# Down groups of 8, 4, 4, 8, 8 tiles, weights split ahead of a stage's end, and a third ordinary pair in the third MLP

## Chip, cores and metric

The kernel runs on one core of one Trainium2 chip. The metric is device time in microseconds, the median of several executions.

## The reference, cut to what matters

Three transformer blocks follow one another on a sequence of 1024 tokens with 1024 channels, all in float32. The change touches the MLP of the first and of the third block, what stands just ahead of the third one, and the small product `w_ada` that runs beside the first one's down projection:

```
# block 1
h = h + square(relu(rms_norm(h, norm_mlp_w) @ w_up)) @ w_down        # 1024 -> 4096 -> 1024
# block 3
mod = silu(c) @ w_ada + b_ada                                        # 6 vectors of 1024, from w_ada (1024, 6144)
x = x + gate1 * rms_norm(mix, norm1_post)
h = rms_norm(x, norm2_pre) * (1 + scale2) + shift2
f = square(relu(h @ w_fc1)) @ w_fc2                                  # 1024 -> 4096 -> 1024
x = x + gate2 * rms_norm(f, norm2_post)
```

## The kernel before

Channels lie on the 128 partitions and tokens along the rows, so that an activation is eight tiles k of 128 x 1024. A weight tile of 128 x 1024 produces 128 output channels. Each float32 product is made of three products of split operands: with `hi` the operand rounded by ScalarE (ACT) and `lo` the rest, TensorE sums hi*hi, hi*lo and lo*hi. For weights ACT writes `whi` (`highs`, a list in the order of use; L1404) from `raw`, and GpSimd (POOL) writes `wlo` in the place of `raw` (`lows`, L3043). `whi` has two buffers, `raw` four.

**The engines' queues** are written out by hand, one function for each engine. An instruction that waits holds up everything behind it in its function. `behind(name)` on SyncE (SP) loads the weights four ahead, once TensorE has released the buffer.

**Up projection of both MLPs.** The 32 tiles of the hidden layer come as 16 pairs (`pair_of`). The first pairs are ordinary ones (`job`): a tile is 8 k x 6 = 48 matmuls of 512 columns, a pair 96. The other pairs are fast ones (`fast`, L746 to L748): a product of 2 x 2 blocks with seven block products p1, p5, p6, p4, p7, p2, p3 instead of eight, 84 matmuls. The fast pairs need sums of activations, made once (operands p5, p6, p4, p7: `operands1`, `operands2`, `operand_lows`), and sums of weights for each pair (`fast_sums` on DVE, `fast_hi` on ACT, `fast_lo` on GpSimd, L3113). Results are put together by `fast_step` on DVE, squared on ACT and written to memory (`spill`, tensor `hsc`). Before, pairs 0 and 1 are ordinary in both MLPs. `drain` multiplies an ordinary tile by the norm's factor RT and squares it on DVE; in the third MLP a `relu` with a bias on ACT stands between. PSUM has three slots of 128 x 1024 in turn, and a fourth tile `misc` for sums and for the norms' factors.

**Down projection** (`down`, `dn` in block 1, `fa2_` in block 3). The 32 hidden tiles are taken in five groups of `SIZES` = 8, 8, 8, 4, 4 tiles. For each group there are eight steps, one for each output tile, so 40 steps n. A step is 48 matmuls in a group of 8 and 24 in a group of 4; DVE adds its result to X. Even groups stand in GH/GL, odd ones in HH/HL. During a group's steps the next group's tiles come back from memory, one in a step (`next_tile`): SP issues `reload`, ACT makes the high half (`high_down`), GpSimd the low half. On ACT the step's order is the weights of step n + 1 and then the high half of the reloaded tile; on GpSimd it is the same. The first group's tiles are reloaded during the last fast pair; their low halves 0, 2, 4, 6 are made by GpSimd, 1, 3, 5, 7 by DVE (`low_down`), 5 and 7 of them behind the last `fast_step`.

**The product with w_ada** runs beside the first MLP's down steps. `ADAS[n]` lists the rows (of 48) that step n carries: two in each of the first 24 steps. A row is a DMA of 512 KB into one of three buffers, eight dependent DVE operations of 128 x 128 (`row_step`, L2475 and L2110) and one small matmul, which TensorE issues a step later. SP's order is

```
for n in range(40):
    ...
    down("up", n)
    for f in ADAS[n]:
        if f + 3 < 48:
            row_load(f + 3)        # waits for "red ada f", the end of row f on DVE
```

and `down` issues the reload of step n, then the weights of step n + 4, which wait for TensorE's end of step n.

**The end of the first MLP.** Behind its last down step follows tile gg0 of the second block, whose weights ACT splits behind the squares of `on_last3` (`behind("gg0")`).

**The start of the third MLP.** `halves` runs fa1_0, fa1_1, fa1_2 in two halves of 512 tokens, with the sums of squares (`sums_half`, L769) and the transposes that spread the factors (`spread_half`, L776) between. Behind them follow the sums and both spreads of norm `nx`, then fa1_3, then the fast pairs. On DVE all operands of the fast pairs are made between the norm's last sum and `factors_half("nx", 1)` (L2916).

Of the kernel before, what the change touches and what calls it, by code (L numbers as in the profile page):

```python
# [16 lines left out]
P = 128  # L17
# [257 lines left out]
def build(nc, d, out):  # L275
    ctx = ExitStack()
    with ctx:
# [164 lines left out]
        ring = [name for name in cut if name != "fa1_1" and name not in SPLIT]  # L442
        ridx = {name: i for i, name in enumerate(ring)}
        WX = at("WX", RO, [P, 1024], R)
        HXF, HF, GF = unit("HXF", HO, 0, [P, 8, S]), unit("HF", HO, 8, [P, 8, S]), unit("GF", GO, 8, [P, 8, S])
# [8 lines left out]
        def whi_of(name):  # L454
            n = int(np.prod(wl[widx[name]][1].shape[1:]))
            if name == "fa2_4_7":
                return whi[ridx[name] % 2][:, n:2 * n]
# [4 lines left out]
            return (WX if name == "fa1_1" else whi[ridx[name] % 2])[:, 0:n]  # L462

# [22 lines left out]
        def wh_of(t, w):  # L486

            return at_whi[(ridx[f"{t}2"] + w % 4 // 2) % 2][w % 2]
# [9 lines left out]

        def corners(t, n):
# [4 lines left out]
        def hidden(n):  # L504

            return TB[2 * (n % 2)], TB[2 * (n % 2) + 1]
# [122 lines left out]
        def tensor(e):  # L629
# [35 lines left out]
            def begin(name, hi, lo, toks, nk, k0=0, m=P, ks=None, between=None):  # L665
# [9 lines left out]
                def step(n):  # L675
# [21 lines left out]
                    elif n == 3 and name in ("up3", "fa1_3"):  # L697
# [29 lines left out]
            def fast(t, n):  # L727
# [3 lines left out]
                for j, p in enumerate(PARTS):  # L731
# [7 lines left out]
                    elif n > 2:  # L739
                        q.wait_ge(*dv({"p1": f"{t}c11 {n - 1}", "p5": f"{t}c12a {n - 1}", "p6": f"{t}u3 {n - 1}", "p4": f"{t}c21a {n - 1}"}[p]))  # L740
                    wh, wl_ = wh_of(t, 7 * (n - 2) + j), part(t, n, p)[1]
                    for k in range(4):
                        if n == 2 and p in OAT:
# [8 lines left out]
            def fast_all(t):  # L752
# [3 lines left out]
                for n in range(2, 16):  # L756
# [587 lines left out]
            def next_norm(name, hf, k):  # L1344
# [5 lines left out]
                elif (name, hf, k) == ("fa1_0", 1, 4):  # L1350
                    sums_half("nx", 0, 0, dv("nx acc7 h0"), dv("mixn 7 0"))

            halves(["fa1_0", "fa1_1", "fa1_2"], hhs, hls, lambda k, hf: [dv(f"hl6 {k} {hf}")], 8, between=next_norm, along=True)
            sums_half("nx", 1, 512, dv("nx acc7 h1"), dv("mixn 7 1"))
            spread_half("nx", 0, misc, dv("nx r1 h0"))
            spread_half("nx", 1, misc, dv("nx r1 h1"))

            def tail(name, hf, k):
# [3 lines left out]
                elif (name, hf, k) == ("fa2_4_6", 1, 1):  # L1362
                    spread_half("nf", 0, misc, dv("nf r1 h0"))

            job("fa1_3", hhs, hls, lambda k: [], 8)
# [3 lines left out]
            halves(["fa2_4_5", "fa2_4_6", "fa2_4_7"], ghs, gls, lambda k, hf: [either(f"fa2_l {FIRST[4] + k}")], 4, between=tail)  # L1369
# [10 lines left out]
        def scalar(e):  # L1380
# [5 lines left out]
            def highs(upto):  # L1386

                while todo and widx[todo[0]] <= upto:
# [3 lines left out]
                    if name == "fa1_1":  # L1392
                        q.wait_ge(*dv("zu3"))
                    elif name == "fa2_4_7":
                        q.wait_ge(*pe("fa2_4_3"))
# [91 lines left out]
            def fast_hi(t, w):  # L1487

                n, p = w // 7 + 2, PARTS[w % 7]
# [7 lines left out]
                if w > 3:  # L1497
                    q.wait_ge(*pe(f"{t}{(w - 4) // 7 + 2} {PARTS[(w - 4) % 7]}"))
                else:
                    q.wait_ge(*pe(f"{t}2" if w < 2 else f"{t}3"))  # L1500
                e.activation(wh_of(t, w), part(t, n, p)[0], ACT.Copy).then_inc(*ac.inc(f"{t}hi {n} {p}"))  # L1501

            def spilled(t, f):

                return dma[f"h{f % 4}"](f"{t}h {f}")

            def fast_s(t, n):

                q.wait_ge(*pe(f"{t}{n} p1"))
                q.wait_ge(*spilled(t, 2 * n - 3))  # L1510
                e.activation(hidden(n)[1][:, 1, :], corners(t, n)[0], ACT.Copy).then_inc(*ac.inc(f"{t}s {n}"))

            def fast_square(t, n, hf, bias):

                x, f = hidden(n)[hf], 2 * n + hf
# [12 lines left out]
            def fast_all(t, bias=None):  # L1528

                for w in range(4):  # L1530
                    fast_hi(t, w)
                for n in range(2, 16):
                    for j in range(7):
                        if 0 < 7 * (n - 2) + j < 95:
                            fast_hi(t, 7 * (n - 2) + j + 3)
                        if n > 2 and j == 0:
                            fast_square(t, n - 1, 1, bias)
                        elif j == 1:
                            fast_s(t, n)
                            if n > 2:  # L1540
# [496 lines left out]
            for hf in range(2):  # L2037
                h = half(hf)
                for k in range(8):
# [4 lines left out]
                    elif (k, hf) == (5, 0):  # L2044
                        root_half("nm", 1, 512)
                    elif (k, hf) == (7, 1):
# [1605 lines left out]
```

## Time and profile before

| | |
|---|---|
| median of 3 runs | 3451.27 us (3446.87 to 3453.66) |
| the profiled execution | 3446.94 us, span 3444.9 us |
| TensorE (PE) busy | 3349.0 us, 97% of the span, 16490 matmuls |
| DVE, ACT, POOL busy | 52%, 33%, 36% |
| mean granted TensorE clock | 0.987 of full speed |

The span runs from the first to the last instruction. PE is TensorE's matmuls, DVE is VectorE, ACT ScalarE, POOL GpSimd, SP SyncE, which issues the DMAs; L746 is line 746 of the kernel. In a timeline each row has its start and its duration in us; durations of pipelined instructions overlap, so that the distance of starts is their cost.

### The profile page before, as it was taken

How to read it: one execution, taken by the hardware profiler on the slowest of the kernel's cores; microseconds unless marked ns; L12 is line 12 of the kernel's file. 1: busy time of each engine (PE TensorE's matmuls, PEld its weight loads, DVE VectorE, ACT ScalarE, POOL GpSimd, SP SyncE). 2: the span in 40 equal slices, each digit the busy share in tenths (PEclk: the TensorE clock that was granted, in tenths of full speed). 3: DMA queues.
4: the chain of work that ended last, by engine and by line, in shares of the span. 5: the costliest groups of instructions: out<-in, count | busy, mean ns of one | idle time of the engine just before them, and what ended most of it. 6: DMA issues, size and time to landing. Idle time of an engine off the chain costs nothing.

```text
span 3444.9 us, 39484 instructions
## 1 busy us (share of the span) xinstructions
PE 3349.0 (97%) x16490; PEld 2723.8 (79%) x16490; DVE 1800.6 (52%) x2283; ACT 1123.6 (33%) x1657; POOL 1253.7 (36%) x682
## 2 busy tenths in 40 slices
PE   8999999999999899999999999999999979999998
PEld 6887888887888778765788888888888758878887
DVE  4653466556664568486445445445555566550114
ACT  5432233332111321485332222212333444452113
POOL 2212325555443222313323344444222335554433
PEclk9999999999999999999999999999999989999999
DMA  2112313226543211220212132222211123242223
GB/s 106 44 50 68 122 49 117 110 110 224 182 175 104 92 68 49 74 60 1 86 45 66 62 98 80 77 89 83 87 43 43 72 81 120 101 165 98 98 69 133
DMA packets 102749, 310.06 MB, mean 90 GB/s; under 512 B 14614, under 2 KB 21542, under 8 KB 102444
## 3 DMA queue, kind: packets, MB, share of 16 engines
q1 hardware_dynamic: 102572, 307.55, 25.6%
q8 instruction: 130, 2.13, 0.2%
q14 instruction: 47, 0.39, 0.0%
HBM read 255.96 MB, written 51.55 MB: 89 GB/s over the span
## 4 chain that ended last, share of the span: by engine, by line
PE 92%; DVE 5%; ACT 2%; POOL 1%; issue 0%; DMA 0%; POOLq 0%; SPq 0%; DVEq 0%; ACTq 0%
PE ps L689 23%; PE ps L690 22%; PE ps L692 22%; PE ps L746 5%; PE ps L748 5%; PE ps L747 5%; PE ps L900 1%; PE ps L1124 1%; DVE T L2107 1%; PE ps L1173 1%; PE ps L1157 1%; DVE P L2634 1%; ACT T L1777 1%; PE ps L1110 0%; POOL wlo L3043 0%; PE ps L1088 0%
## 5 line engine op out<-in xcount | busy, mean ns | idle before, releaser
L3043 POOL TENSOR_TENSOR wlo<-raw,whi 128x1024 fp32r<-128x1024 f32 (+4 forms) x261 | 555.8, 2130 | 1390.9 <-ACT whi L1404 1390.9
L689 PE MATMUL ps<-HH,whi 128*128 128x512 f32 (+2 forms) x2224 | 880.6, 396 | 15.9 <-POOL wlo L3043 9.5
L690 PE MATMUL ps<-HL,whi 128*128 128x512 f32 (+2 forms) x2224 | 870.5, 391 | 0.0
L692 PE MATMUL ps<-HH,wlo 128*128 128x512 f32 (+2 forms) x2224 | 688.6, 391 | 0.0
L1404 ACT ACTIVATE whi<-raw 128x1024 fp32r<-128x1024 f32 (+4 forms) x261 | 237.8, 912 | 1013.0 <-PE ps L692 867.9
L689 PEld LDWEIGHTS ps<-HH,whi 128*128 128x128 f32 (+2 forms) x2224 | 416.9, 187 | 108.7 <-DVE mod L2107 9.9
L692 PEld LDWEIGHTS ps<-HH,wlo 128*128 128x128 f32 (+2 forms) x2224 | 416.4, 187 | 92.5 <-issue 1.1
L690 PEld LDWEIGHTS ps<-HL,whi 128*128 128x128 f32 (+2 forms) x2224 | 416.8, 187 | 89.4 <-issue 2.2
L2107 DVE TENSOR_TENSOR X<-ps,X 128x1024 f32<-128x1024 f32 (+1 forms) x139 | 166.8, 1201 | 588.8 <-PE ps L692 585.1
L689 PE MATMUL ps<-GH,whi 128*128 128x512 f32 x1096 | 431.3, 394 | 0.6 <-POOL wlo L3043 0.6
L690 PE MATMUL ps<-GL,whi 128*128 128x512 f32 x1096 | 426.7, 389 | 0.0
L692 PE MATMUL ps<-GH,wlo 128*128 128x512 f32 x1128 | 349.2, 391 | 0.0
L2118 DVE TENSOR_TENSOR T<-ps,RT 128x1024 f32<-128x1024 f32 x72 | 88.2, 1225 | 311.1 <-PE ps L692 267.7
L692 PEld LDWEIGHTS ps<-GH,wlo 128*128 128x128 f32 x1128 | 212.8, 189 | 45.0
L689 PEld LDWEIGHTS ps<-GH,whi 128*128 128x128 f32 x1096 | 205.9, 188 | 42.9 <-POOL wlo L3043 1.0
L690 PEld LDWEIGHTS ps<-GL,whi 128*128 128x128 f32 x1096 | 205.9, 188 | 41.4
L3113 POOL TENSOR_TENSOR wlo<-raw,whi 128x512 fp32r<-128x512 f32 x112 | 164.6, 1471 | 160.6 <-ACT whi L1501 152.1
L2107 DVE TENSOR_TENSOR T<-T,ps 128x512 f32<-128x512 f32 (+1 forms) x118 | 84.0, 712 | 201.7 <-PE ps L748 169.5
L746 PE MATMUL ps<-OHp,whi 128*128 128x512 f32 x448 | 174.6, 390 | 0.0
L747 PE MATMUL ps<-OLp,whi 128*128 128x512 f32 x448 | 174.5, 389 | 0.0
L2110 DVE SCALAR_TENSOR_TENSOR T<-T,cols,T 128x1023 f32<-128x1023 f32 x88 | 126.9, 1442 | 62.1 <-ACT T L1905 60.5
L746 PE MATMUL ps<-HH,whi 128*128 128x512 f32 x336 | 131.8, 392 | 5.0 <-POOL wlo L3113 5.0
(450 smaller groups left out, 4909.3 us busy)
## 6 DMA issues: line engine op xcount, KB each, us to landing
raw<-in_w_fc SPq DMA_DIRECT2D x88, 512.0 KB, 3.4
raw<-in_w_up SPq DMA_DIRECT2D x76, 512.0 KB, 3.3
raw<-in_w_in SPq DMA_DIRECT2D x70, 512.0 KB, 3.2
hsc<-T SPq DMA_DIRECT2D x50, 512.0 KB, 2.6
GF<-hsc SPq DMA_DIRECT2D x40, 512.0 KB, 5.3
T<-in_w_ada SPq DMA_DIRECT2D x32, 512.0 KB, 4.1
raw<-in_w_down SPq DMA_DIRECT2D x56, 256.0 KB, 2.7
raw<-in_w_down SPq DMA_DIRECT2D x24, 512.0 KB, 5.0
```

What stands on the lines that cost most here:

```text
L689: e.matmul(o_[0:m, half(hf)], whi_[k], hi[k0 + k][:, half(hf)], start=first, stop=False)
L690: e.matmul(o_[0:m, half(hf)], whi_[k], lo[k0 + k][:, half(hf)], start=False, stop=False)
L692: i = e.matmul(o_[0:m, half(hf)], wlo_[k], hi[k0 + k][:, half(hf)], start=False, stop=last)
L746: e.matmul(bank[p], wh[:, blk(k)], hi, start=k == 0 and p not in ("p2", "p7", "p3"), stop=False, skip_group_check=True)
L747: e.matmul(bank[p], wh[:, blk(k)], lo, start=False, stop=False, skip_group_check=True)
L748: i = e.matmul(bank[p], wl_[:, blk(k)], hi, start=False, stop=k == 3, skip_group_check=True)
L1404: e.activation(whi_of(name), v3(raw_of(name), 2) if name in SPLIT else raw_of(name), ACT.Copy).then_inc(*ac.inc("hi " + name))
L2107: e.tensor_tensor(o, a, b, op).then_inc(*dv.inc(*names))
L2110: e.scalar_tensor_tensor(out=o, in0=a, scalar=s_, in1=b, op0=op0, op1=op1).then_inc(*dv.inc(*names))
L2118: e.tensor_tensor(dst, ps[slot[g]][:], RT[:], MUL).then_inc(*dv.inc("free " + g, *names))
L3043: e.tensor_tensor(wlo_of(name), raw_of(name), whi_of(name).bitcast(F), SUB).then_inc(*po.inc("lo " + name))
L3113: e.tensor_tensor(o, x, wh_of(t, w).bitcast(F), SUB).then_inc(*po.inc(f"{t}lo {n} {p}"))
```

## The change

It does five things.

1. The down groups of both MLPs have 8, 4, 4, 8, 8 tiles. The w_ada rows are spread anew: two in steps 0 to 7, one in steps 8 to 23, two in steps 24 to 31. The last three tiles of the third MLP, run in halves, have 8 products in k instead of 4.
2. The weights of gg0 are split by ACT and GpSimd at step 39 of the first MLP's down projection, ahead of the squares of the last tiles.
3. DVE's low halves 5 and 7 stand ahead of the last two `fast_step`s.
4. In the third MLP the sums of the norm's second half stand inside fa1_1, the factors directly behind `operands1`, the spreads ahead of and inside fa1_3, whose weights get a buffer of their own (WY) and are split earlier. fa1_0 is copied from PSUM to SBUF by ACT. The operands p6, p4, p7 and the low halves are made between the drains of the ordinary tiles, in the order p5, p6, p4, p7.
5. The third MLP has three ordinary pairs, and the squares of their tiles move from DVE to ACT.

```diff
-ADAS = [[2 * n, 2 * n + 1] if n < 24 else [] for n in range(40)]
+ADAS = [[2 * n, 2 * n + 1] if n < 8 else [n + 8] if n < 24 else [2 * n - 16, 2 * n - 15] if n < 32 else [] for n in range(40)]
-SIZES, FIRST = [8, 8, 8, 4, 4], [0, 8, 16, 24, 28]
-FAST = {f"{t}{f}" for t in DN for f in range(4, 32)}
+SIZES, FIRST = [8, 4, 4, 8, 8], [0, 8, 12, 16, 24]
+ORD = {"up": 2, "fa1_": 3}
+FAST = {f"{t}{f}" for t in DN for f in range(2 * ORD[t], 32)}
...
# TensorE
+                elif (name, hf, k) == ("fa1_1", 1, 7):
+                    sums_half("nx", 1, 512, dv("nx acc7 h1"), dv("mixn 7 1"))
             halves(["fa1_0", "fa1_1", "fa1_2"], hhs, hls, lambda k, hf: [dv(f"hl6 {k} {hf}")], 8, between=next_norm, along=True)
-            sums_half("nx", 1, 512, dv("nx acc7 h1"), dv("mixn 7 1"))
             spread_half("nx", 0, misc, dv("nx r1 h0"))
-            spread_half("nx", 1, misc, dv("nx r1 h1"))
...
-            job("fa1_3", hhs, hls, lambda k: [], 8)
+            job("fa1_3", hhs, hls, lambda k: [], 8, between=lambda k: k == 2 and spread_half("nx", 1, misc, dv("nx r1 h1")))
+            for f in range(4, 2 * ORD["fa1_"]):
+                job(f"fa1_{f}", hhs, hls, lambda k: [], 8)
...
# ScalarE, down()
                 if n < 39:
                     highs(following(t, n))
+                elif t == "up":
+                    highs(widx["gg0"])
...
# ScalarE, third MLP
+            q.wait_ge(*pe("fa1_0"))
+            q.wait_ge(*dv("nx acc7 h1"))
+            e.activation(T[0][:], ps[slot["fa1_0"]][:], ACT.Copy).then_inc(*ac.inc("fa1_c0", "free fa1_0"))
+            root_half("nx", 1, 512)
             for i in range(4):
-                operands2("fa1_", i)
-            highs(widx["fa1_3"])
-            root_half("nx", 1, 512)
+                high(f"fa1_o5f {i}", OF["p5"][:, i, :], OF["p5"][:, i, :], dv(f"fa1_o5d {i}"), scale=gains[:, 16 + i:17 + i])
...
+            def fa1_square(f):
+                q.wait_ge(*ac(f"fa1_r{f}"))
+                e.activation(T[f % 3][:], T[f % 3][:], ACT.Square).then_inc(*ac.inc(f"fa1_s{f}"))
+            for f in range(3):
                 relu(f)
+                fa1_square(f)
+                high(f"fa1_o5h {f}", OF["p5"][:, f, :], OH["p5"][:, f, :])
+            high("fa1_o5h 3", OF["p5"][:, 3, :], OH["p5"][:, 3, :])
+            highs(widx["fa1_4"])
+            for i in range(4):
+                high(f"fa1_o6h {i}", OF["p6"][:, i, :], OH["p6"][:, i, :], dv(f"fa1_o6f {i}"))
+            relu(3)
+            fa1_square(3)
+            highs(widx["fa1_5"])
...
# DVE, fast_all()
                     if n == 15:
                         low_down(t, 3)
+                        low_down(t, 5)
+                        low_down(t, 7)
                     fast_step(t, n, "p4", bias)
                     fast_step(t, n, "p3", bias)
-                low_down(t, 5)
-                low_down(t, 7)
...
# DVE, third MLP
             operands1("fa1_")
-            for i in range(4):
-                operands2("fa1_", i, fc_gain)
-                if i:
-                    operand_lows("fa1_", i - 1)
-            operand_lows("fa1_", 3)
             factors_half("nx", 1)
...
+            for i in range(4):
+                fresh("p6", i)
             q.wait_ge(*ac("nx rt"))
-            for f in range(4):
-                if f == 3:
-                    fast_sums("fa1_", 2)
+            for f in range(3):
                 drain("fa1_", f, True)
+            for i in range(4):
+                fresh_low("p5", i)
+            for i in range(4):
+                fresh("p4", i)
+            drain("fa1_", 3, True)
+            for i in range(4):
+                fresh("p7", i)
+                fresh_low("p6", i)
+            drain("fa1_", 4, True)
+            for i in range(4):
+                fresh_low("p4", i)
+            fast_sums("fa1_", 3)
+            drain("fa1_", 5, True)
```

`fresh(p, i)` is one DVE operation of 128 x 512 (X times its gain, less the operand before), `fresh_low` the subtraction of the high half.

## Rows read from the trace of the kernel before

**Rows 1.** TensorE's waits, whole span: total us, times, longest us.

```profile
PE ps L776 <- DVE rms L2916: 18.4, 2, 17.8
PE ps L689 <- POOL wlo L3043: 10.1, 2, 9.5
...
PE ps L689 <- DVE GL L2107: 6.8, 3, 3.6
```

**Rows 2.** TensorE's timeline, the two ends of the first MLP's down stage.

```profile
797.99 0.61 PE L692 MATMUL ps<-GH,wlo 128*128 128x512 f32 x2
...
807.26 0.39 PE L689 MATMUL ps<-GH,whi 128*128 128x512 f32 x1
...
1156.17 0.61 PE L692 MATMUL ps<-GH,wlo 128*128 128x512 f32 x2
...
1171.28 0.40 PE L689 MATMUL ps<-HH,whi 128*128 128x512 f32 x1
```

**Rows 3.** TensorE's timeline, third MLP (in brackets: idle before, and what ended it).

```profile
2763.33 0.95 PE L769 MATMUL ps<-ones,T 128*128 128x1 f32 x8
...
2785.63 0.80 PE L689 MATMUL ps<-HH,whi 128*128 128x512 f32 x1 [1.95 <-DVE T L2107]
...
2803.27 0.76 PE L746 MATMUL ps<-HH,whi 128*128 128x512 f32 x1 [4.97 <-POOL wlo L3113]
...
2825.27 0.39 PE L746 MATMUL ps<-HH,whi 128*128 128x512 f32 x1
...
2827.99 0.39 PE L746 MATMUL ps<-OHp,whi 128*128 128x512 f32 x1
...
3079.29 0.61 PE L692 MATMUL ps<-GH,wlo 128*128 128x512 f32 x2
3083.49 0.80 PE L689 MATMUL ps<-GH,HH 128*128 128x512 f32 x1 [3.58 <-DVE GL L2107]
...
3090.38 0.40 PE L689 MATMUL ps<-GH,whi 128*128 128x512 f32 x1
...
3417.32 0.47 PE L721 MATMUL ps<-GH,whi 128*128 128x512 f32 x1 [0.38 <-POOL wlo L3043]
```

**Rows 4.** ACT's timeline at the start of the third MLP.

```profile
2765.04 5.29 ACT L1471 ACTIVATE OHp<-OFp 128x512 fp32r<-128x512 f32 x10
...
2785.61 1.15 ACT L2072 ACTIVATE T<-T,pbias 128x1024 f32<-128x1024 f32 x1 [1.29 <-DVE T L2107]
```

**Rows 5.** DVE's and GpSimd's timelines at the start of the third MLP.

```profile
2777.53 4.90 DVE L2107 TENSOR_TENSOR OLp<-OFp,OHp 128x512 fp32r<-128x512 f32 x8
...
2779.30 5.33 POOL L3043 TENSOR_TENSOR wlo<-raw,whi 128x1024 fp32r<-128x1024 f32 x1 [21.45 <-ACT whi L1404]
```

**Rows 6.** DMA landings and GpSimd, first MLP, steps with 4 tiles.

```profile
GF<-hsc SPq DMA_DIRECT2D x4, 512.0 KB, 4.2
...
1077.33 1.31 POOL L3043 TENSOR_TENSOR wlo<-raw,whi 128x512 fp32r<-128x512 f32 x1
```

**Rows 7.** DVE, GpSimd, SP (its DMA queue) and ACT, down steps with two rows.

```profile
909.33 1.23 DVE L2107 TENSOR_TENSOR X<-ps,X 128x1024 f32<-128x1024 f32 x1 [6.08 <-PE ps L692]
...
910.86 2.49 DVE L2110 SCALAR_TENSOR_TENSOR adat<-T,SC,adat 128x128 f32<-128x128 f32 x1
913.27 2.48 DVE L2110 SCALAR_TENSOR_TENSOR adat<-RT,SC,adat 128x128 f32<-128x128 f32 x1
915.68 0.34 DVE L2110 SCALAR_TENSOR_TENSOR adat<-T,SC,adat 128x128 f32<-128x128 f32 x1
...
910.72 2.48 POOL L3049 TENSOR_TENSOR GL<-GF,GH 128x1024 fp32r<-128x1024 f32 x1 [2.55 <-ACT GH L1471]
...
918.68 0.33 SPq L3274 DMA_DIRECT2D T<-in_w_ada  x1
...
919.53 0.43 SPq L3274 DMA_DIRECT2D GF<-hsc  x1
...
925.41 1.06 ACT L1471 ACTIVATE GH<-GF 128x1024 fp32r<-128x1024 f32 x1 [13.82 <-DMA GF<-hsc]
```

More of the change, by code:

```diff
@@ L439, in build @@
         cidx = {name: i for i, name in enumerate(cut)}
-        ring = [name for name in cut if name != "fa1_1" and name not in SPLIT]
+        ring = [name for name in cut if name not in ("fa1_1", "fa1_3", "fa2_4_7") and name not in SPLIT]
         ridx = {name: i for i, name in enumerate(ring)}
         WX = at("WX", RO, [P, 1024], R)
+        WY = at("WY", GO + 16384, [P, 1024], R)
         HXF, HF, GF = unit("HXF", HO, 0, [P, 8, S]), unit("HF", HO, 8, [P, 8, S]), unit("GF", GO, 8, [P, 8, S])
@@ L461, in whi_of @@
                 return HH[:, 0:2, half(1)]
-            return (WX if name == "fa1_1" else whi[ridx[name] % 2])[:, 0:n]
+            return (WX if name == "fa1_1" else WY if name == "fa1_3" else whi[ridx[name] % 2])[:, 0:n]
         def wlo_of(name):
@@ L497, in operand @@
             return HH[:, k, half(h)], HL[:, k, half(h)]
+        WAS = {t: [f"{t}{f}" for f in range(2 * ORD[t]) if f"{t}{f}" in ridx][-2:] for t in DN}
         def corners(t, n):
@@ L502, in corners, with hidden, earlier, last_tx @@
             return xz[:, half(0)], xz[:, half(1)], yw[:, half(0)], yw[:, half(1)]
-        def hidden(n):
-            return TB[2 * (n % 2)], TB[2 * (n % 2) + 1]
+        def hidden(t, n):
+            i = (n - ORD[t]) % 2
+            return TB[2 * i], TB[2 * i + 1]
+        def earlier(t, n, hf):
+            m = ORD[t]
+            if n > m + 1:
+                return 2 * n - 4 + hf
+            return None if (n, hf) == (m, 0) else max(f for f in range(2 * m) if f % 3 == {(m, 1): 1, (m + 1, 0): 2, (m + 1, 1): 0}[n, hf])
+        def last_tx(t):
+            return dma["h0" if ORD[t] == 2 else "h2"](f"{t}h 28" if ORD[t] == 2 else f"{t}h 30")
+        def spilled(t, f):
+            return dma[f"h{f % 4}"](f"{t}h {f}")
         def next_tile(n):
@@ L696, in step @@
                         i.then_inc(*pe.inc("zu3 late"))
-                    elif n == 3 and name in ("up3", "fa1_3"):
+                    elif n == 3 and name in [pair_of(t, ORD[t] - 1)[1] for t in DN]:
                         i.then_inc(*pe.inc(name + " half"))
@@ L755, in fast_all @@
                 take(t + " yw")
-                for n in range(2, 16):
+                for n in range(ORD[t], 16):
                     fast(t, n)
@@ L1368, in tensor @@
                 down("fa1_", n)
-            halves(["fa2_4_5", "fa2_4_6", "fa2_4_7"], ghs, gls, lambda k, hf: [either(f"fa2_l {FIRST[4] + k}")], 4, between=tail)
+            halves(["fa2_4_5", "fa2_4_6", "fa2_4_7"], ghs, gls, lambda k, hf: [either(f"fa2_l {FIRST[4] + k}")], 8, between=tail)
             q.wait_ge(*ac("nf sd h0"))
@@ L1528, in fast_all @@
             def fast_all(t, bias=None):
-                for w in range(4):
+                for w in range(2 if bias else 0, 4):
                     fast_hi(t, w)
-                for n in range(2, 16):
+                m = ORD[t]
+                for n in range(m, 16):
                     for j in range(7):
-                        if 0 < 7 * (n - 2) + j < 95:
-                            fast_hi(t, 7 * (n - 2) + j + 3)
-                        if n > 2 and j == 0:
+                        if 0 < 7 * (n - m) + j < 7 * (16 - m) - 3:
+                            fast_hi(t, 7 * (n - m) + j + 3)
+                        if n > m and j == 0:
                             fast_square(t, n - 1, 1, bias)
@@ L2434, in fast_all @@
             def fast_all(t, bias=False):
-                for n in range(2, 16):
+                for n in range(ORD[t], 16):
                     if n < 15:
@@ L3115, in fast_all @@
             def fast_all(t):
-                for w in range(98):
-                    if w == 95:
+                m = 7 * (16 - ORD[t])
+                for w in range(m):
+                    if w == m - 3:
                         lows(following(t, -1))
@@ L3127, in down @@
                     lows(following(t, n))
+                elif t == "up":
+                    lows(widx["gg0"])
                 if next_tile(n):
@@ L3252, in gpsimd @@
                     lows(widx["fa1_2"])
+                elif n == 7:
+                    lows(widx["fa1_3"])
             for n in (1, 3, 5, 7):
```

101 lines of the change are left out of this document (66 added, 35 removed).

## Prediction

> **What bounds the kernel now.** I read the list of what TensorE waited for first, then TensorE's own timeline around each of those waits, then the timelines of the other four engines in the same stretches. TensorE is busy for 97% of the span, so time can only come from its waits and from the number of its matmuls. Steady work costs 2.72 us for 12 matmuls of 512 columns, the distance of two parts of one pair [rows 3], or 0.227 us each. The longest waits lie where stages meet [rows 1], and every wait of nearly 3 us or more is followed by matmuls at half the clock. So I count a wait as time lost between two rows of the timeline, less the matmuls between them.
>
> **The four seams before.** (a) First MLP, up to down: between 797.99 and 807.26 stand 20 matmuls (4.53 us), so 9.27 - 4.53 = 4.7 us are lost [rows 2]. (b) First MLP to the second block: 14 matmuls (3.17 us) between 1156.17 and 1171.28, 11.9 us lost [rows 2]. (c) Start of the third MLP: from 2763.33 to 2825.27 TensorE has one ordinary tile, one fast pair (48 + 84 matmuls, 29.9 us) and some 1.6 us of sums and spreads to do, and takes 61.9 us: 30.4 us lost [rows 3]. (d) Third MLP, up to down: 20 matmuls between 3079.29 and 3090.38, 6.6 us lost [rows 3].
>
> **(b), weights of gg0 split ahead.** The ACT copy and the GpSimd subtraction now run during the last down tile (10.9 us with 8 tiles in its group). The data is no obstacle: of X only k = 7 comes late. DVE works on for five operations of 1.23 us, like the X added at 909.33 [rows 7], after the last matmul before that operand is ready (x, low half, two sums, low half: 6.2 us), and TensorE asks for k = 7 only 7 x 1.36 = 9.5 us in. The sums behind gg0 are due at 10.9 us and DVE ends at about 8.5. Gain 11.9; if something else is late by the old 2 us, 9.5.
>
> **(a) and (d), low halves 5 and 7 ahead of the last two products.** The wait named GL [rows 1] is for them. They now stand before the p4 and p3 steps. I take (a) whole, 4.7, and of (d), where the reloads land later, 6.0: GpSimd and DVE take turns there, and what is late next is the slot of the second down tile, freed by the p3 step. That could give back 3 us.
>
> **(c), the third MLP.** Now the sums of the second half run inside the last tile, `factors_half` comes right behind `operands1`, and fa1_0 is copied out of PSUM by ACT, so fa1_3 starts at about 2764.6 and ends 11.3 us later, at 2775.9. What is late next is fa1_4's weights. On ACT they stand behind three times relu, square and one high half, and one more. The factor RT is ready at 2768.5 (its transposes stand at k = 2 of fa1_3), the first product 1.2 later, at 2769.7. A relu takes 1.15 and its square about 1.0 behind it [rows 4], a high half 0.52 (ten in 5.29 [rows 4]): 3 x 2.67 + 0.52 = 8.5, so the weights' high half runs 2778.3 to 2779.3. GpSimd's low half then wants its inputs while DVE streams four differences of 0.7 (estimate: the eight of rows 5 are 0.6 apart, and these multiply as well), until 2781.9. The only row of this kind is the same operation at 2779.30: 5.33 us, beside eight DVE operations without a gap, ending only 2.2 us after the last of them [rows 5]. So it ends at 2781.9 + 2.2 = 2784.1: a new wait of 8.2 us, plus 1.9 us of slow clock. By the Trainium skill ("SBUF — State Buffer", Who interferes with whom) whichever instruction starts first has the shared port for that one instruction; by this GpSimd would wait for one DVE operation only, end at about 2782.3, and the gain would be 1.8 us larger; the row of 5.33 us says otherwise. From there fa1_4 ends at 2796.9 and fa1_5 at 2807.8, with operands, sums and the first part's weights in time by 2 us; then at most 0.5 us for the p6 weights. The pair behind starts at 2807.8 + 0.5 where before it started at 2825.27: gain 17.0, in which the 12 matmuls more of an ordinary pair (96 against 84, 2.7 us) are already paid. If DVE's PSUM product doesn't let GpSimd in, its stream runs on to 2789 and the gain is 10 to 12; if GpSimd isn't held off at all, 19.
>
> **Tail.** The second half of the last three tiles is twice as long, so DVE is done with the first outputs and the wait of 0.4 us for weights [rows 3] goes. I take 1.0.
>
> Sum of the gains: 4.7 + 11.9 + 17.0 + 6.0 + 1.0 = 40.6 us; bounds 32 and 44.
>
> **Down groups of 8, 4, 4, 8, 8.** The matmuls are the same. What changes is what shares a step. Before, the first MLP's groups of 4 had no `w_ada` rows beside them. Now the 16 steps of groups 1 and 2 have one row each, and 12 of these steps also reload a tile for the next group. Each is 24 matmuls and a row, 5.44 + 0.25 = 5.69 us. SyncE is one queue: in step n it issues the reload, waits for the end of the matmuls, then waits for DVE's reduction before it fetches the next row, and only behind that comes the next reload. Before, with two rows a step, this is visible: X at 909.33, the row loads held to 918.68, the reload at 919.53, its high half on ACT at 925.41 [rows 7]. ACT in turn splits the weights of tile n + 2 behind that high half, and GpSimd their low half behind the tile's. So from the start of step n to the earliest start of step n + 2: X added 1.15; eight dependent operations on the row, 8 x 0.38 = 3.0 (estimate: a free one takes 0.34 [rows 7], and with one row each waits for the one before); SyncE 0.45; landing 5.0 (4.2 with only 256 KB ahead [rows 6], 5.9 with two rows ahead [rows 7]); ACT with hand-overs 1.2; GpSimd 2.4 [rows 7] + 1.3 [rows 6]. That is 14.5, against 2 x 5.69 = 11.4. Six pairs of steps lose 3.1 each, 18.6 us, and the slow clock after the last stall of either group adds up to 4.
>
> That is without a clash of DVE and GpSimd. At 910.86 and 913.27 a row operation took 2.5 us instead of 0.34, the first beside GpSimd's 2.48 from 910.72 [rows 7]. In the new loop GpSimd's 3.7 us begins 10.6 us after a step's start, and the next step's row work lies 8.4 to 11.2 us after it: in every other step the row ends 3 to 4 us late and so does the next reload. Walking through the twelve steps with these terms gives 16 to 16.5 us for two steps instead of 14.5, thus 5 x 6 = 30 us lost in all. The same walk over the old groups gives no wait, as in the trace. I take 30. Bounds: 9 with the shortest terms (row 2.1, landing 4.2, no clash: 12.9 a pair), and 62 if every step's row is held (POOL 3.7, rest of the row 0.6, SyncE 0.45, landing 4.9, ACT 1.2: 10.9 a step). The third MLP has no rows: its reload is issued at the step's start and 0.4 + 4.3 + 1.2 + 3.7 = 9.6 is under 10.9, no loss. By the Trainium skill ("TensorE: Matmul & The Clock Gate", HAM oscillation) a loop with a wait in every round pays a slow restart in every round; with the 1.9 us of (c) for each of six stalls that would be 11 us, but here the reload chain, not TensorE, sets the pace, and hides most of it.
>
> **Sum.** -40.6 + 30 = -10.6. The profiled execution took 3446.94 (span 3444.9 and 2 around it), so 3436.3 by its own time; that is as short as the shortest of the three runs, and their median is 3451.27, 4.3 above. 10.6 below the median is 3440.7. I predict 3439, between the two. A measurement of this kernel can tell about 0.2%, 7 us, from no change.
>
> **Rivals.**
> 1. No clash: DVE's rows slip between GpSimd's operations. Loss 18.6, net -22, 3429. For it: a single row is short, and alternate steps start early. Against: the blocked operation of 2.49 us. Chance 0.2.
> 2. The rows hide altogether (the reload isn't held). Net -40.6, 3411. Against: SyncE's order in the rows of before. Chance 0.07.
> 3. The other side: every step's row is caught behind GpSimd, 10.9 us a step, loss 62. Its place is steps 8 to 11 and 16 to 23; it decides from a loss of 41, a step of 9.1 us. Net +21, 3472. For it: two of DVE's operations in a row were held for the length of one GpSimd operation each. Against: the steps fall apart into a long and a short one, and after the long one DVE is free. Chance 0.09.
> 4. (c) gives only 10, as GpSimd is held off until 2789, the rest as forecast: net -4, 3447, no measurable change. Chance 0.14.
>
> The forecast has 0.5; its own range is 3432 to 3447. Range over the cases: 3420 to 3453, which leaves out rivals 2 and 3. Faster by over 0.2%: most of the forecast (0.43), rivals 1 and 2: 0.69. Within 0.2%: 0.07 + 0.14 = 0.21. Slower: rival 3 and a little: 0.1.
>
> **What would show it.** In the profile of the changed kernel: no wait for wlo at gg0; a stretch of first down steps 8 to 23 that takes some 120 us instead of 91, with TensorE waiting for GpSimd's wlo by 3 to 4 us about six times and reloads issued right behind row loads; at the third MLP no wait for the factors, but one of about 8 us for fa1_4's wlo; no GL wait at the start of either down stage beyond 1 us; steps of 5.44 us in the third MLP's groups of 4. Wrong it would be if the 4-tile steps of the first MLP run at 5.7 us, or if the weights of fa1_4 are there at 2776.

## The result, and the profile after

The changed kernel takes 3460.03 us (median of 9 runs, 3456.43 to 3464.34), the kernel before 3451.27 (9 runs, 3446.87 to 3453.68). The ratio is 1.0032, 95% interval 1.0023 to 1.0041: slower by 0.3%, where 0.3% faster was predicted. The profiled execution took 3459.79 us, span 3458.0, against 3444.9 before: 13.1 us more, where the medians are 8.8 apart, since the profiled execution of the kernel before was one of its shortest and that of the changed kernel lies at its median.

TensorE's waits over the whole span (total us, times, longest), in the changed kernel; compare [rows 1]:

```profile
PE ps L710 <- POOL wlo L3125: 37.1, 11, 7.2
...
PE ps L742 <- POOL wlo L3125: 4.9, 1, 4.9
...
PE ps L990 <- DVE adat L2163: 2.1, 3, 1.1
```

The long waits for GL and for the factors (rms) are gone, and where there were two waits for split weights (wlo) in the ordinary matmuls there are eleven. (The single wait of 4.9 us, at 2750.66, lies just ahead of the third MLP. Experiment 3, which leaves that place as it was, has one of 4.72 there, experiment 1 has none, and in all three the norm's sums behind it come 0.8 to 1.0 us later than in the kernel before, counted from the transposes of the second block.) TensorE's timeline shows where they lie:

```profile
815.71 0.65 PE L990 MATMUL ps<-ones,adat 128*128 128x1 f32 x4 [1.09 <-DVE adat L2163]
820.48 0.80 PE L710 MATMUL ps<-GH,whi 128*128 128x512 f32 x1 [4.12 <-POOL wlo L3125]
832.83 0.50 PE L990 MATMUL ps<-ones,adat 128*128 128x1 f32 x4
...
1199.66 1.84 PE L841 MATMUL ps<-ones,T 128*128 128x1 f32 x16
...
1214.63 1.03 PE L862 MATMUL ps<-ident,rms 128*128 128x128 f32 x8
...
2807.73 0.77 PE L710 MATMUL ps<-HH,whi 128*128 128x512 f32 x1 [6.22 <-POOL wlo L3125]
2832.20 0.39 PE L767 MATMUL ps<-HH,whi 128*128 128x512 f32 x1
2844.18 0.47 PE L767 MATMUL ps<-OHp,whi 128*128 128x512 f32 x1 [0.61 <-DVE HF L2160]
...
3081.08 0.39 PE L710 MATMUL ps<-GH,HH 128*128 128x512 f32 x1
...
3111.88 0.79 PE L710 MATMUL ps<-GH,whi 128*128 128x512 f32 x1 [7.17 <-POOL wlo L3125]
3267.58 0.47 PE L710 MATMUL ps<-HH,whi 128*128 128x512 f32 x1 [0.65 <-POOL wlo L3125]
```

Profiled executions of the variants below reach the first down stage at 789 to 800 us, though nothing ahead of it differs. So I compare distances between the same marks of the timeline, not times since the start. A mark is a place that both programs have: the start of a stage, the first w_ada row matmuls, the norm's sums.

| stretch | before | after | change | forecast |
|---|---|---|---|---|
| first down stage, first three tiles | 37.88 | 41.05 | +3.2 | -4.7 |
| from there to the sums behind gg0 | 349.96 | 366.83 | +16.9 | +18.1 |
| those sums to the next transposes | 11.79 | 14.97 | +3.2 | 0 |
| to pair 3 of the third MLP | 1634.00 | 1617.57 | -16.4 | -17.0 |
| pair 3 to the third MLP's down stage | 247.68 | 248.88 | +1.2 | 0 |
| down stage to the tail's sums, and the tail | 360.43 | 365.40 | +5.0 | -7.0 |

With 0.1 us ahead of them the rows add up to +13.1. The last stretch holds the same number of matmuls in both. Its part up to the tail's sums takes 349.90 before and 349.82 after, but has 24 matmuls (5.4 us) fewer after the change; so 5.4 us are lost there, and the tail itself gains 0.4. The down groups' own stretch, as the windows of the changed kernel show it (length; then busy time of PE, its weight loads, DVE, ACT, POOL; granted clock; DMA share; GB/s):

```profile
890.06:1010.38 120.32, 100.99 (x420) 81.88 (x420) 89.90 (x152) 20.87 (x27) 47.45 (x27) 0.91 0.44 160
...
1199.66:1214.63 14.97, 14.97 (x70) 12.86 (x68) 1.07 (x6) 1.63 (x3) 2.35 (x1) 0.77 0.01 2
```

Steps 8 to 23 take 120.3 us; "some 120" was forecast. Of the 29.3 us above 91.0, TensorE stands idle for 19.3, and its 420 matmuls take 101.0 us at a granted clock of 0.91, where experiment 10 has 91.8 at 1.00. The surprises are the two starts of the down stages. The engines' timelines of the changed kernel there (DVE, SP's DMA queue, ACT, GpSimd):

```profile
791.95 9.53 DVE L2160 TENSOR_TENSOR GL<-GF,GH 128x1024 fp32r<-128x1024 f32 x3
801.40 0.67 DVE L2160 TENSOR_TENSOR T<-T,ps 128x512 f32<-128x512 f32 x1
...
803.91 1.66 SPq L3361 DMA_DIRECT2D hsc<-T  x2
...
808.65 0.38 SPq L3361 DMA_DIRECT2D HF<-hsc  x1
...
814.53 1.06 ACT L1496 ACTIVATE HH<-HF 128x1024 fp32r<-128x1024 f32 x1 [9.31 <-DMA HF<-hsc]
815.49 1.04 ACT L1429 ACTIVATE whi<-raw 128x1024 fp32r<-128x1024 f32 x1
...
818.09 2.34 POOL L3125 TENSOR_TENSOR wlo<-raw,whi 128x1024 fp32r<-128x1024 f32 x1
```

Read it downwards: three low halves on DVE, which take 1.2 us each in the kernel before when GpSimd is idle, take 9.5 beside GpSimd's; the product behind them starts at 801.4; the spill of the last pair, the first reload for the next group, its high half, and only then the weights of the third tile follow, each waiting for the one above. The same chain in the kernel before, where DVE made one low half ahead of the products:

```profile
791.81 2.83 DVE L2107 TENSOR_TENSOR GL<-GF,GH 128x1024 fp32r<-128x1024 f32 x1
...
798.58 3.11 SPq L3274 DMA_DIRECT2D hsc<-T  x2
...
804.73 0.38 SPq L3274 DMA_DIRECT2D HF<-hsc  x1
...
811.50 1.05 ACT L1404 ACTIVATE whi<-raw 128x1024 fp32r<-128x1024 f32 x1
...
814.97 2.40 POOL L3043 TENSOR_TENSOR wlo<-raw,whi 128x1024 fp32r<-128x1024 f32 x1
```

There the reload goes out 3.9 us earlier, and the weights are ready at 817.37, 1.1 us before TensorE asks for them at 818.51. After the change they come 3.1 us later and TensorE, which no longer waits for GL, asks 2.1 us earlier: 3.1 + 2.1 - 1.1 is the new wait of 4.1 us. In the third MLP one link more has come in:

```profile
3095.14 0.33 SPq L3361 DMA_DIRECT2D hsc<-T  x1
3097.27 0.53 SPq L3361 DMA_DIRECT2D hsc<-HF  x1
3102.24 0.33 SPq L3361 DMA_DIRECT2D HF<-hsc  x1
```

With three ordinary pairs the last pair's result lies in HF (`hidden(t, n)` counts from `ORD[t]`), the buffer into which the reload goes, and so the reload waits for the spill to land: 5.0 us between the last two rows.

### The profile page after: what moved, and what is told of

The parts are those of the page before. It is cut to its first block, busy times and chain, and to the rows that moved or that the text cites. A ratio compares the mean times of both kernels' runs of the same rounds, so it can differ in the third digit from the quotient of the medians.

```text
span 3458.0 us, 39464 instructions
## 1 busy us (share of the span) xinstructions
PE 3361.3 (97%) x16502; PEld 2732.0 (79%) x16502; DVE 1820.0 (53%) x2268; ACT 1125.2 (33%) x1656; POOL 1254.0 (36%) x677
## 4 chain that ended last, share of the span: by engine, by line
PE 89%; DVE 5%; ACT 3%; DMA 1%; POOL 1%; issue 0%; SPq 0%; POOLq 0%; DVEq 0%; ACTq 0%
PE ps L710 22%; PE ps L711 22%; PE ps L713 22%; PE ps L767 5%; PE ps L769 5%; PE ps L768 5%; PE ps L921 1%; DVE GL L2160 1%; PE ps L1145 1%; DMA HF<-hsc 1%; POOL wlo L3125 1%; PE ps L742 1%; PE ps L744 1%; PE ps L743 1%; PE ps L1194 1%; DVE T L2160 1%
## 5 line engine op out<-in xcount | busy, mean ns | idle before, releaser
L710 PE MATMUL ps<-HH,whi 128*128 128x512 f32 (+2 forms) x2240 | 891.1, 398 | 19.9 <-POOL wlo L3125 15.5
L711 PE MATMUL ps<-HL,whi 128*128 128x512 f32 (+2 forms) x2240 | 879.6, 393 | 0.0
L713 PE MATMUL ps<-HH,wlo 128*128 128x512 f32 (+2 forms) x2256 | 701.2, 392 | 0.0
L710 PEld LDWEIGHTS ps<-HH,whi 128*128 128x128 f32 (+2 forms) x2240 | 422.1, 188 | 114.0 <-issue 10.8
L713 PEld LDWEIGHTS ps<-HH,wlo 128*128 128x128 f32 (+2 forms) x2256 | 424.2, 188 | 94.5 <-issue 1.1
```

Of the source, the lines that this page charges most:

```text
L710: e.matmul(o_[0:m, half(hf)], whi_[k], hi[k0 + k][:, half(hf)], start=first, stop=False)
L711: e.matmul(o_[0:m, half(hf)], whi_[k], lo[k0 + k][:, half(hf)], start=False, stop=False)
L713: i = e.matmul(o_[0:m, half(hf)], wlo_[k], hi[k0 + k][:, half(hf)], start=False, stop=last)
```

## The experiments

Each ratio is to the kernel before, measured on the same chip. The stretches are read from one execution of each kernel; where that one is far from the median, the text says so.

**1. The old groups** (SIZES 8, 8, 8, 4, 4 and two rows in each of 24 steps; the tail's halves with 4 products).

> The changed kernel with the old down groups (8, 8, 8, 4, 4) and the old two rows a step, all else as changed. In the changed kernel's trace steps 8 to 23 take 120.3 us instead of 91.0. If the groups and the rows in them cost that and nothing else: 29.3 us less, the profiled execution at about 3431, the ratio to the kernel before about 0.994 to 0.996; the waits at 820.5 and at the second down tile of the third MLP stay. Rival: the late start of the first group (820.5) also feeds the stalls behind it, or the tail's gain is worth more than the 0.4 us that I read; then the steps give under 25 us. By the prediction's own terms for everything else it would be 3404 to 3410; the trace of the changed kernel speaks against that already.

3430.18 us, ratio 0.9947 (0.9934 to 0.9959). The groups and the rows in them cost what the stretch shows, 29 to 30 us; the waits at the two third tiles stay (4.12 and 6.29 us).

**2. Low halves 5 and 7 behind the products again.**

```diff
                         low_down(t, 3)
-                        low_down(t, 5)
-                        low_down(t, 7)
                     fast_step(t, n, "p4", bias)
                     fast_step(t, n, "p3", bias)
+                low_down(t, 5)
+                low_down(t, 7)
```

> The changed kernel with the low halves 5 and 7 behind the last two products again, as before the change. Theory (the late spill): the three low halves in a row hold the products by 4.1 us, so the last spill, the reload behind it and the weights split behind the reload are late at both down stages. Undone, the wait of 4.1 us in the first MLP (820.5) goes and the wait for GL (3.0, and 1.7 of slow clock) comes back: 3.2 us gained there; in the third MLP the wait of 7.2 us goes and GL's 3.6 comes back: about 5.3. In all 8 to 9 us less, 3451. Rival (the slot in the third MLP): there the reload also waits for the landing of a spill out of HF, so a wait of 2 to 3 us stays besides GL's and the third MLP gives only 1 to 3: 3454 to 3456. If the order of the low halves has nothing to do with the weights: the waits stay and GL's are added, 3467.

3449.77, ratio 1.0004 (0.9995 to 1.0013): 10 us less than the changed kernel. The first three tiles take 37.60 (41.05), the third MLP's stretch up to the tail's sums 343.80 (349.82); both waits for the third tile's weights are gone and GL's (2.83 and 3.54 us) are back. These two places give 9.5 us. Steps 8 to 23, which this edit leaves alone, took 116.4 us this time, and this profile reached the first down stage 4.0 us later than the changed kernel's.

**3. The same move alone, in the kernel before.**

> The kernel before with this one part of the change alone: low halves 5 and 7 ahead of the last two products. The prediction said 4.7 + 6.0 = 10.7 us less. Theory of the late spill: in the first MLP the gain of 4.7 turns into a loss of 3 (a wait of 4 us at the third tile); in the third MLP, where the last pair lies in T and the reload needs no landing of that spill, the weights of the third tile were 5 us early before, so 6.5 are gained and 2 to 5 given back. Together between 2 less and 2 more than before, ratio 0.9994 to 1.0006. If the ratio is under 0.998, the theory is wrong.

3458.45, ratio 1.0023 (1.0014 to 1.0032). Slower, where no measurable change was expected: the first three tiles 41.37 (37.88 before), the third MLP's stretch 351.95 (349.90). There, where the last pair lies in T, the third tile waits 3.88 us. Another 3.2 us of its trace are the sums behind gg0, told below. So the loss in both stages comes from this one move, and it's larger than I had worked out.

**4. Weights ahead of the reloaded tile** in the first four steps of each down stage, on ACT and GpSimd.

```diff
                 if n < 39:
-                    highs(following(t, n))
+                    highs(following(t, n + 1 if n < 4 else n))
```

(and the same for `lows`).

> The changed kernel, in which ACT and GpSimd split the weights of the tile after next ahead of the reloaded tile in the first four steps of both down stages, so that the weights no longer stand behind the late reload. Theory of the late spill: the waits of 4.1 us (first MLP) and 7.2 us (third MLP) for wlo and the slow clock behind them, 1.3 and 2.5, go: 13 to 15 us less, about 3446, and the 4.7 and most of the 6.0 us that were forecast appear at the seams. Rival 1: a row of w_ada is the next thing late in the first MLP (its load stands behind the same spill), 1 to 3 us come back there. Rival 2: the two engines are late in themselves, not through the reload; then the waits stay.

3442.49, ratio 0.9982 (0.9973 to 0.9990): 17.5 us less than the changed kernel. The first three tiles take 35.22 us, the third MLP's stretch 339.98. TensorE has 33.0 us of work in the former (144 matmuls and a pair of rows), and a wait of 0.9 for the first row (rival 1) stays. The low half of the third tile's weights starts at 806.22, where it was 818.09.

**5. The reload one step ahead of the rows** in SP's queue, steps 9 to 23.

```diff
                 behind("{}{}_{}".format(DN[t], *divmod(n, 8)))
+                if ahead and n % 8 < 7 and next_tile(n + 1):
+                    fetch(n + 1)            # the reload of step n + 1
```

> The changed kernel, in which SyncE issues the reload of step n+1 ahead of the rows of step n in steps 9 to 23 of the first MLP (first reload of each group in its place). Theory of the prediction (the reload waits in SyncE's queue behind the row, and the whole chain hangs on it): the stretch of steps 8 to 23 falls from 120.3 to 91 to 98 us, the kernel to about 3432 to 3438. Rival (DVE and GpSimd, not the queue): a step needs 1.15 for X and 3.0 for the row on DVE, and DVE is held for up to 3.7 us of GpSimd's work, 7.9 us against 5.7 in each of the 12 steps with a reload; then the stretch stays above 110 us.

3458.52, ratio 1.0028 (1.0019 to 1.0036). No gain that can be told: the stretch took 117.8 us, and the profiles of experiments 2, 4, 7 and 8, which leave these steps as the change has them, give 116.4 to 120.7. But the reload now stood behind the weights' load, which waits for a step's end, so this was not yet a test of the queue.

**6. No rows in steps 8 to 23** (a third of the rows is left out).

> The changed kernel without the rows of w_ada in steps 8 to 23: 16 of the 48 rows are left out (not loaded, not multiplied; their columns of the modulation get those of other rows). Both theories of the stalls say that they go: 16 x 5.44 = 87 us for the steps, 33 us less than now, about 3427. If groups of 4 tiles stall without rows as well (reload 0.4, landing 4.3, ACT 1.2, GpSimd 3.7 in a row), the stretch stays above 92 us.

3439.67, ratio 0.9973 (0.9963 to 0.9983). The stretch takes 96.6 us, not 87: one stall of 5.1 us (at 910.67) and its slow clock stay, ahead of step 10. (The profiled execution, 3444.56 us, was the longest of the eight; whether the others have the whole stall isn't shown.) Its weights are split behind the reload of step 8, and that stands in SP's queue behind the two rows of step 7.

**7. No wait for the spill's landing** (reloads of tiles 0 and 1, third MLP).

```diff
-reload(t, f, k, 1 - to_g, pe(f"{t}15 p3"), last_tx(t), ...)
+reload(t, f, k, 1 - to_g, pe(f"{t}15 p3"), *([last_tx(t)] if n > 1 or t == "up" else []), ...)
```

> The changed kernel, in which the reloads of tiles 0 and 1 of the second group in the third MLP no longer wait until the spill of the last pair has landed (these two tiles lie elsewhere in HF than that pair). In the trace of the changed kernel the spill is issued at 3097.3 and the reload at 3102.2. Theory (three orders pair 15 into HF, so the reload has to wait for its landing, 4.9 us that the kernel before did not have): the wait of 7.2 us for the third tile's weights falls to 2 to 3, and with the slow clock 5 to 7 us are gained, 3453 to 3455. Rival (the late products alone): the wait stays above 5 us, no measurable change.

3458.06, ratio 1.0028 (1.0019 to 1.0038), no measurable change. In the trace the wait falls from 7.17 to 4.60 us and the stretch from 349.82 to 346.63. The reload goes out at 3108.62, right behind the spill at 3108.00, but then it takes 5.5 us to arrive instead of 3.8. So the landing is worth some 3 us, the late products the other 4. (The profiled execution, 3467.34 us, was the longest of its ten, but it was 8 us late before the first down stage. The other profiles with this place as the change has it wait 6.1 to 7.8 us, all longer than 4.60.)

**8. fa1_4's and fa1_5's high halves earlier on ACT**: ahead of the three relus and squares, and where fa1_4's was.

> The changed kernel with ACT's high half of the weights of fa1_4 ahead of the three relu and squares, and that of fa1_5 where fa1_4's was. In the changed kernel's trace the high half runs at 2803.7, behind three relu and squares, and TensorE waits 6.2 us for the low half. Theory (the order on ACT is the cause): the weights are ready by 2798, fa1_4 starts right behind fa1_3, and 6 to 7.5 us are gained, 3452 to 3454, ratio 1.001. Rival: DVE's work for pair 3 (operands and products, all shifted by 1 us) is the next thing late, and pair 3 starts no more than 3 us earlier.

3450.61, ratio 1.0002 (0.9993 to 1.0011): 9.4 us less by the medians. Pair 3 starts 1610.99 us behind the transposes of the second block, where it was 1617.57: 6.6 us, and what waits there now is 0.3 us.

**9. Reloads two steps ahead**, the first two of a group right at the end of the group before, ahead of that step's rows.

```diff
                 behind("{}{}_{}".format(DN[t], *divmod(n, 8)))
+                if t == "up" and 7 <= n < 23:
+                    for m in ((n + 1, n + 2) if n % 8 == 7 else (n + 2,) if n % 8 < 6 else ()):
+                        if next_tile(m):
+                            fetch(m)
```

> In the run with the reload one step ahead it still stood behind the weights' load, which waits for the end of a step, and landed 6.3 us after its issue, so the chain was not cut. Here, in steps 7 to 22 of the first MLP, SyncE issues each reload two steps ahead, and the first two of a group right at the end of the group before, ahead of that step's rows; all else as in the changed kernel. Theory of the prediction (the reload's chain through SyncE's queue): all stalls of steps 8 to 23 go, the stretch falls from 120 to 91 to 98 us, the kernel to 3432 to 3438. Rival (DVE and GpSimd): the stall of 5 us with its slow clock at the first step of the groups of 4 goes, 7 to 8 us, but every step with a reload and a row still needs about 7.3 us (X 1.15, row 3.0, and 3.1 for which DVE is held beside GpSimd's 3.7), as so many steps do in the runs so far: 12 x 1.6 = 19 us stay lost, the stretch at 110, the kernel at about 3450.

3466.17, ratio 1.0052 (1.0039 to 1.0065): slower still. The windows of steps 8 to 23 for this kernel, 124.0 us, above all of the 116.4 to 120.7 seen so far:

```profile
891.21:1015.20 123.99, 102.62 (x420) 82.20 (x420) 100.83 (x153) 23.12 (x29) 52.93 (x29) 0.90 0.47 159
```

And its GpSimd and DVE at the start of that stretch:

```profile
896.77 2.56 POOL L3131 TENSOR_TENSOR GL<-GF,GH 128x1024 fp32r<-128x1024 f32 x1 [3.66 <-ACT GH L1496]
899.30 1.28 POOL L3125 TENSOR_TENSOR wlo<-raw,whi 128x512 fp32r<-128x512 f32 x1
900.55 2.44 POOL L3131 TENSOR_TENSOR GL<-GF,GH 128x1024 fp32r<-128x1024 f32 x1
903.87 1.27 POOL L3125 TENSOR_TENSOR wlo<-raw,whi 128x512 fp32r<-128x512 f32 x1 [0.88 <-ACT whi L1429]
905.43 2.44 POOL L3131 TENSOR_TENSOR GL<-GF,GH 128x1024 fp32r<-128x1024 f32 x1 [0.30 <-ACT GH L1496]
...
899.46 8.55 DVE L2163 SCALAR_TENSOR_TENSOR adat<-RT,SC,adat 128x128 f32<-128x128 f32 x7
```

Seven operations of a row take 8.55 us while GpSimd runs beside them; TensorE then waits for the row's result (5.0 us at 908.07).

**10. As 9, with the reloaded tile's low half on DVE** behind the row, steps 8 to 23.

> The kernel with the reloads early, and with the low half of the reloaded tile in steps 8 to 23 on DVE behind the row, where GpSimd did it. GpSimd's 2.4 us go, DVE gets one operation of 1.2 more. If the reload's chain sets the pace, no difference to the run with the reloads early (2.4 of GpSimd become 1.2 of DVE, but behind the row), or it gets slower. If DVE held beside GpSimd sets it: a step needs 1.15 + 3.0 + 1.2 and at most 1.3 beside the weights' low half, 5.4 to 6.6 instead of 7.3; 8 to 19 us less than the run with the reloads early, 3431 to 3442.

3432.01, ratio 0.9952 (0.9939 to 0.9966): 34 us less than kernel 9. The windows of steps 8 to 23, and a row of DVE's timeline:

```profile
890.78:983.40 92.62, 91.82 (x420) 75.78 (x420) 85.41 (x163) 23.25 (x29) 21.86 (x16) 1.00 0.63 213
```

```profile
898.73 2.68 DVE L2163 SCALAR_TENSOR_TENSOR adat<-RT,SC,adat 128x128 f32<-128x128 f32 x7
901.33 1.22 DVE L2160 TENSOR_TENSOR GL<-GF,GH 128x1024 fp32r<-128x1024 f32 x1
```

Seven operations take 2.68 us again, every step but the first (6.16, with two rows) and the last (6.76) takes 5.69, and the clock is whole.

**11. The low half on DVE alone**, the reloads where the change has them.

> The changed kernel with the reloads where the change has them, and the low half of the reloaded tile in steps 8 to 23 on DVE behind the row: the other half of the last run's edit alone. It tells whether the place of the reload in SyncE's queue costs anything once GpSimd's 2.4 us are gone. If only GpSimd's low half held the steps: the stretch takes 92 to 94 us as with both edits, the kernel 3432. If the queue matters too: two steps need X 1.15, row 3.0, SyncE 0.45, landing 5.0, ACT 1.2 and the weights' low half 1.3 = 12.1 against 11.4, 4 us over six pairs, and the stall at the entry, 8 us in the run without rows, stays: the stretch 100 to 105, the kernel 3440 to 3445.

3446.58, ratio 0.9989 (0.9980 to 0.9998). Both numbers that I had given were too small:

```profile
895.35:1004.86 109.51, 97.10 (x421) 79.65 (x420) 85.11 (x165) 20.75 (x27) 25.48 (x16) 0.95 0.53 186
```

With most of the clash gone, 109.5 us are left, and TensorE's five waits there (1.7 to 3.6 us) are all for GpSimd's wlo, which hangs on the reload: this is the chain through SP's queue. Why it costs 18.5 us and not the 9 to 14 of my estimate stays open; one link that I had left out is that DVE now waits for the reloaded tile too, ahead of the next row. The profiled execution, 3456.87 us, was the longest of the eleven, 10.3 above the median. By the medians the kernel is 13.5 us shorter than the changed one, where the stretch gives 10.8, so the usual execution may lose less than 18.5 here.

**12. The parts that pay, together**: the changed kernel with edits 1, 4, 7 and 8.

> The changed kernel with the old groups and rows, the weights ahead of the reloaded tile in the first four steps of both down stages, the reloads of tiles 0 and 1 in the third MLP without the wait for the spill's landing, and the weights of fa1_4 and fa1_5 earlier on ACT. If the parts add: 3460 - 29.5 (groups) - 15.6 (weights ahead) - 6.6 (fa1_4) = 3408, ratio 0.988. The reload without the landing adds nothing once the weights are ahead of it. Rival: the earlier start shifts a wait to the third MLP's next seam or to a row, and 5 to 10 us are given back, 3413 to 3418.

3408.01, ratio 0.9882 (0.9869 to 0.9896): 1.2% faster than the kernel before. The parts add as they should: first three tiles 35.3 us, the way to the sums behind gg0 338.1 (11.9 less than before), pair 3 24.9 us earlier, the third down stage 345.0 (4.9 less).

## Why the prediction was wrong

**(a) and (d), the low halves: wrong in sign.** The step that failed is "what is late next is the slot of the second down tile". I looked at what TensorE waits for and asked which slot comes free, not at what follows the delayed products on the other engines. The last product ends 3.9 us later (804.12 where it was 800.24), and on the products hang the squares, the spill, the first reload, ACT's high half, and behind it the weights of the third tile. That chain had 1.1 us to spare in the first MLP. Forecast -4.7, measured +3.2. Undoing the move (experiment 2), making it alone (3) and taking the weights out of the chain (4) each moved it the way the chain says. In the third MLP the same chain holds 5 us more, because pair 15 now lies in HF; forecast -6.0, measured +5.4. Experiments 3 and 7 split its wait of 7.2 us: 3.9 with the late products alone (in the kernel before), 2.6 less without the landing. With the weights ahead (experiment 4) most of the forecast gains is there: against the kernel before 2.7 us in the first MLP and 4.5 in the third.

**Groups and rows: the size right, 29.3 us against 30, in part by luck.** Its working had two terms, the reload's chain through SP's queue (18.6) and the clash of DVE and GpSimd on top (to 30). Two edits, each alone and both together, show that both exist. Steps 8 to 23, which need 91 us:

| | GpSimd makes the low half | DVE makes it |
|---|---|---|
| reload behind the rows | 120.3 | 109.5 |
| reload two steps ahead | 124.0 | 92.6 |

With the queue and little of the clash 18.5 us are lost. That this is rival 1's number is chance: its chain still had GpSimd's 2.4 us in it. Without the queue but with the clash it is 33. So the two don't add up: the clash alone fills the stretch, the queue alone fills 60% of it, and taking out one lets the other show. That is why experiment 9 found no gain, and it would have misled had it been the last. What was luck in the size: the working had six equal losses of 5 us. In the trace the first loss, 7.5 us ahead of step 10, has a cause that it did not name, the reload of step 8 behind the two rows of step 7: a wait of the same length stays when the rows of steps 8 to 23 are gone (experiment 6). The other steps lose 21.8. The slow clock behind the stalls, put at up to 4 us, makes 9.2 of the 29.3 (101.0 less 91.8). Where six waits of 3 to 4 us were listed, five of 2.6 to 5.0 came, in irregular steps; TensorE's wait for a row (adat), up to 6.3 us with early reloads, was not foreseen.

**(b), gg0: right at its seam.** No wait for gg0's weights; the stretch of 384 matmuls up to the sums takes 87.17 us (87.04 of work), 12 us gained. That the sums and the tile behind them took 3.2 us longer needs no part of the change: in experiment 3, which leaves that place as it was before, they take 14.97 as well. Experiments 1 and 6 show 15.0, the other nine 13.4, and the kernel before 11.79 in its one profile. The granted clock goes with it: 0.77 at 14.97, 0.87 at 13.38 (experiment 5), 1.00 at 11.79. What decides between these stays open.

**(c), third MLP: right in size, 16.4 against 17.0**, of which 0.8 is lost before it. All there lies 24.2 us later than before. Less that, pair 3 starts at 2808.0, where 2808.3 was forecast. The wait for fa1_4's weights is 6.2 us, not 8.2: fa1_3 ended 1.4 later than forecast, and two errors in the weights' chain nearly cancelled. ACT's high half ended 1.3 later, and the term "ends at 2781.9 + 2.2", GpSimd held off by DVE, was wrong:

```profile
2804.63 4.83 DVE L2163 SCALAR_TENSOR_TENSOR OFp<-X,gains,OFp 128x512 f32<-128x512 f32 x4
...
2804.86 2.72 POOL L3125 TENSOR_TENSOR wlo<-raw,whi 128x1024 fp32r<-128x1024 f32 x1 [21.06 <-ACT whi L1429]
```

GpSimd began behind DVE's first operation, took 2.7 us, and DVE's four took 4.8 instead of 2.8: the opposite of [rows 5]. By the Trainium skill ("SBUF — State Buffer", Who interferes with whom) a DVE operation with two inputs in SBUF and a GpSimd one that reads SBUF exclude each other, and the one issued first blocks the other for its whole length. These rows agree, and so do the row operations of experiment 9; [rows 5] alone was a poor guide. What makes the stall is the place of the weights on ACT behind three relus, the first of which starts at 2795.25: experiment 8 put them ahead, and the wait went.

**Tail and 4-tile steps of the third MLP.** The tail gained 0.4, not 1.0. The groups of 4 without rows run at 5.44 us a step but for one wait of 0.65, as forecast.

In all: -10.6 forecast, +13.1 found; (a) is off by 7.9, (d) by 11.4, the sums behind gg0 by 3.2, the rest by 1. The 1.2 us more between pair 3 and the third down stage stay open. Rival 3, the one on the other side, was not what happened: its place was the down groups, and these cost what was forecast.

Two readings of the prediction need correcting. It says that every wait of nearly 3 us or more is followed by matmuls at half the clock. In the kernel before, a wait of 3.10 us at 2637.04 is followed by matmuls 0.23 us apart, the full pace, and in the changed kernel so is the one of 2.91 at 964.83. What a wait costs is read from the rows behind it. And its chances of a faster kernel add up to 0.70, not 0.69.

## What to carry to other kernels

When an engine's work is moved ahead of something, follow what is moved back through every queue to the next thing that TensorE needs, and note the slack of each link, not only the wait that goes. Two causes can fill the same gap: an edit that removes one and gains nothing has not cleared that cause, so try both together. A forecast whose total comes true can still have its parts in the wrong places, so compare it place by place. And where two engines hold each other up, the work may be better on the quicker of the two (1.2 us on DVE against 2.4 on GpSimd, experiment 10).

## What was not expected of the hardware

- Fetching data earlier made the kernel slower by 6 us (experiment 9 against the changed kernel), as GpSimd's operations then ran beside the dependent row operations: 7 of them took 8.55 us instead of 2.68.
- The same 70 matmuls behind gg0 took 11.8, 13.4 or 15.0 us in different profiles; the granted clock in that stretch was 1.00, 0.87 and 0.77. In the changed kernel's profile the 87 us of matmuls just before it had 1.00.
- A reload issued right behind a spill landed after 5.5 us (experiment 7); one issued 5.0 us behind the spill's issue landed after 3.8 (the changed kernel).
